# First attention of a transformer layer: the values become the standing operand, and the probabilities are divided by their sum before they are turned

## The reference, cut to what matters

```python
# group 0: |distance| <= 64; groups 1 and 2: the tokens of the same class (stride 4, stride 16)
sc = where(valid, einsum('qe,ke->qk', q, k) * 64 ** -0.5, -1e30)      # per group, per head
lse = logsumexp(sc); p = exp(sc - lse); o = p @ v                      # per group
o_a = sum_g softmax_g(lse)[g] * o[g]                                   # = one softmax over all groups' keys
# second branch: 8 query heads over 2 key heads, dense over 256 keys
o_b = softmax(q_b @ k_b.T * 64 ** -0.5) @ v_b
merged = sigmoid(gate0 + b0) * (o_a @ w_proj_a) + sigmoid(gate1 + b1) * (o_b @ w_proj_b)
x = x + merged @ w_out
# then rmsnorm, a router (top 4 of 32 experts), and the experts' swiglu
```

## Time and profile before

| what | value |
|---|---|
| median of three runs | 1928.79 us (1928.77 to 1929.28) |
| profiled execution, its own time | 1928.52 us |
| its span, first to last instruction | 1926.7 us |
| PE, DVE, ACT busy | 96%, 48%, 30% of the span |
| granted PE clock | 0.999 |
| read from memory | 558.08 MB, 290 GB/s over the span |

### The profile page before, as it was taken

How to read it: one execution, slowest core, us unless ns; L and a number is a source line. 1 busy time by engine, 2 the same in 40 slices (tenths; PEclk the granted TensorE clock), 3 DMA queues, 4 the chain that set the end, 5 groups by cost and what they waited for, 6 DMA issues and landing times.

```text
span 1926.7 us, 25464 instructions
## 1 busy us (share of the span) xinstructions
PE 1857.3 (96%) x10228; PEld 1110.0 (58%) x10228; DVE 917.1 (48%) x1607; ACT 584.1 (30%) x863; POOL 100.3 (5%) x120
## 2 busy tenths in 40 slices
PE   8999999999999999999999999999999999999998
PEld 5877874333333333233233333787888887878886
DVE  6864465323332333233232232676765455566544
ACT  3554442111111111111111111554435344555432
POOL 2410000000000000000000000020410000000000
PEclk9999999999999999999999999999999999999999
DMA  7543399999999999999999999542145455436452
GB/s 253 175 146 116 112 392 407 417 426 428 426 428 428 427 429 426 429 428 427 429 426 429 427 428 427 184 162 97 60 160 178 171 199 177 151 131 240 153 204 81
DMA packets 106464, 560.29 MB, mean 291 GB/s; under 512 B 5904, under 2 KB 11280, under 8 KB 81808
## 3 DMA queue, kind: packets, MB, share of 16 engines
q1 hardware_dynamic: 102528, 551.61, 71.2%
q10 hardware_dynamic: 3856, 7.53, 1.3%
HBM read 558.08 MB, written 1.05 MB: 290 GB/s over the span
## 4 chain that ended last, share of the span: by engine, by line
PE 71%; DMA 19%; DVE 4%; ACT 3%; issue 2%; POOL 1%; POOLq 0%; SPq 0%; ACTq 0%; DVEq 0%
PE ps L1297 14%; PE ps L948 11%; PE ps L949 11%; PE ps L950 11%; DMA ring<-in_w_gate_up_dram 10%; DMA arena<-in_w_gate_up_dram 8%; PE ps L1327 8%; PE ps L1226 2%; PE ps L1238 2%; PE ps L962 1%; PE ps L1312 1%; PE ps L1557 1%; DVE arena L2862 1%; PE ps L1434 1%; PE ps L984 1%
## 5 line engine op out<-in xcount | busy, mean ns | idle before, releaser
L1297 PE MATMUL ps<-ring,arena 128*64 128x512 f32 x1280 | 286.6, 596 | 23.8 <-DMA ring<-in_w_gate_up_dram 23.8
L2720 DVE TENSOR_SCALAR arena<-ps 128x512 f32<-128x512 f32 x32 | 22.1, 691 | 518.5 <-PE ps L1297 518.5
L2260 DVE TENSOR_TENSOR split_w<-ring,split_w 128x1024 fp32r<-128x1024 f32 (+2 forms) x176 | 203.9, 1205 | 81.9 <-ACT split_w L2054 81.3
L948 PE MATMUL ps<-split_w,act_parts 128*128 128x512 f32 (+1 forms) x544 | 209.7, 386 | 2.0 <-issue 1.0
L1297 PEld LDWEIGHTS ps<-ring,arena 128*64 128x64 f32 x1280 | 87.8, 137 | 209.9 <-issue 161.5
L950 PE MATMUL ps<-split_w,act_parts 128*128 128x512 f32 (+1 forms) x544 | 205.7, 378 | 0.0
L949 PE MATMUL ps<-split_w,act_parts 128*128 128x512 f32 (+1 forms) x544 | 205.3, 377 | 0.0
L2054 ACT ACTIVATE split_w<-ring 128x1024 fp32r<-128x1024 f32 (+2 forms) x176 | 171.7, 1033 | 110.1 <-PE ps L950 108.6
L1297 PE MATMUL ps<-arena 128*64 128x512 f32 x768 | 172.5, 595 | 10.6 <-DMA arena<-in_w_gate_up_dram 10.3
L1327 PE MATMUL ps<-ring,arena 128*64 128x512 f32 x720 | 160.6, 594 | 0.1
L1945 ACT ACTIVATE arena<-arena 128x512 f32<-128x512 f32 x32 | 20.2, 630 | 457.7 <-DVE arena L2720 457.7
(11 more groups left out here) (382 smaller groups left out, 2804.3 us busy)
## 6 DMA issues: line engine op xcount, KB each, us to landing
ring<-in_w_gate_up_dram SPq DMA_DIRECT2D x80, 2048.0 KB, 34.1
arena<-in_w_gate_up_dram SPq DMA_DIRECT2D x48, 2048.0 KB, 27.0
ring<-in_w_down_dram SPq DMA_DIRECT2D x45, 2048.0 KB, 33.7
ring<-in_f_w_dram SPq DMA_DIRECT2D x28, 2048.0 KB, 8.0
arena<-in_w_down_dram SPq DMA_DIRECT2D x19, 2048.0 KB, 37.2
ring<-in_w_in_dram SPq DMA_DIRECT2D x14, 2048.0 KB, 7.8
ring<-in_a_w_in_dram SPq DMA_DIRECT2D x6, 2048.0 KB, 8.1
ring<-in_b_w_qkv_dram SPq DMA_DIRECT2D x6, 2048.0 KB, 8.0
```

The costliest lines, as they stand in the source:

```text
L948: pe.matmul(dst, lh, rh, start=start, stop=False)
L1297: mm = pe.matmul(ps[half, bank, :], xeT[:, 2 * c + j, :], w[:, j, col:col + 512], start=False, stop=(c == 3 and j == 1), skip_group_check= ...
L2260: dve.tensor_tensor(part_place(load, 1, k, n)[:, s_, :], raw_place(load, k, n)[:, s_, :], part_place(load, 0, k, n)[:, s_, :], ALU.subtract)\
L2720: dve.tensor_scalar(gate_c, ps[:, 1, :], 7.0, None, ALU.min).then_inc(m_clipped, 1)
```

## The change

v becomes the standing operand and the turned probabilities the moving one, so the sums come out turned (head dimension on the partitions, queries along the free axis), and the turning after the last step is gone. The inverse of the sums can then no longer be applied to the result; DVE applies it to the probabilities ahead of the turn, in place. ACT takes the high part of each unit's sums and DVE the low part at once. v of groups 1 and 2 is kept so that group 1 fills partitions 0 to 63 and group 2 partitions 64 to 127 (`v_class`), which needs two copies of 64 partitions per tile, and lets one matmul per 64 queries and head cover both groups. The turned results lie in the arena over the place of the early chunk (`once_place`) and in a part of `late`, so these two transfers move behind the output projections. The rows of `w_proj_b` are put in another order on the host.

```diff
@@ sync
-            read_out(sync, G_PROJ - 1)
-            sync.dma_start(once_place, expert_weights(*divmod(ONCE, RING))).then_inc(mask_in, 16)
             load(OUT_LOAD, w_out3[:, :, 0:512])
-            sync.wait_ge(o_turned, 4)
+            sync.wait_ge(pv_done, UNITS)
             expert_chunk(0, 0, 0)
             load(OUT_LOAD + 1, w_out3[:, :, 512:1024])
             sync.wait_ge(pre_split, quarters_done(OUT_LOAD, 3))
             expert_chunk(1, 0, 1)
             sync.wait_ge(gemm_ready, G_PROJ + 8)
             expert_chunk(2, 0, 2)
+            read_out(sync, G_PROJ - 1)
+            sync.dma_start(once_place, expert_weights(*divmod(ONCE, RING))).then_inc(mask_in, 16)
@@ tensor
             def turn_probs(u):
-                pe.wait_ge(probs_ready, u + 1)
+                pe.wait_ge(probs_scaled, u + 1)
...
                 else:
                     for e in range(2):
-                        for j in range(2):
-                            pe.transpose(ps[:, 6 + e, j * P:(j + 1) * P],
-                                         probs_a[:, e, j * P:(j + 1) * P], ident)
-                    for e in range(2):
-                        for g in range(1, NG):
-                            for a in range(2):
-                                own = slice(CLASS * a, CLASS * a + CLASS)
-                                mm = pe.matmul(ps[own, 6 + e, keys_of(g)],
-                                               probs_a[own, e, keys_of(g)], ident[own, own],
-                                               start=True, stop=True, skip_group_check=True)
+                        for j in range(KEYS // P):
+                            mm = pe.transpose(ps[:, 6 + e, j * P:(j + 1) * P],
+                                              probs_a[:, e, j * P:(j + 1) * P], ident)
@@ weighted, dense units
-                    for kv in range(2):
-                        for kt in range(2):
-                            j = 2 * kv + kt
-                            mm = pe.matmul(ps[:, 5, S + 64 * kv:S + 64 * kv + 64],
-                                           probsT[:, j * P:(j + 1) * P],
-                                           v_b[:, kt, 64 * kv:64 * kv + 64], ...)
+                    for kt in range(2):
+                        for kv in range(2):
+                            j, q = 2 * kv + kt, slice(64 * kv, 64 * kv + 64)
+                            mm = pe.matmul(ps[q, 5, S:S + P], v_b[:, kt, q],
+                                           probsT[:, j * P:(j + 1) * P], ...)
@@ weighted, the other units
-                    for e in range(2):
-                        for kt in range(2):
-                            pe.matmul(ps[:, 5, out_at[e]], probsT_a[:, e, kt * P:(kt + 1) * P],
-                                      v_a[:, kt, v_at[e]], ...)
-                        for g in range(1, NG):
-                            for a in range(2):
-                                own = slice(CLASS * a, CLASS * a + CLASS)
-                                mm = pe.matmul(ps[own, 5, out_at[e]], probsT_a[own, e, keys_of(g)],
-                                               v_groups[own, g, v_at[e]], ...)
+                    for kt in range(2):
+                        for e, q in enumerate(head_rows):
+                            pe.matmul(ps[q, 5, S:S + P], v_a[:, kt, v_at[e]],
+                                      probsT_a[:, e, kt * P:(kt + 1) * P], ...)
+                    for a in range(2):
+                        own = slice(S + CLASS * a, S + CLASS * a + CLASS)
+                        for e, q in enumerate(head_rows):
+                            mm = pe.matmul(ps[q, 5, own], v_class[:, tile, a, v_at[e]],
+                                           probsT_a[:, e, own], ...)
@@ behind the last step
-            pe.wait_ge(o_ready, UNITS)
-            for b, o in enumerate((o_b, o_a)):
-                for tile in range(NT):
-                    for j in range(4):
-                        mm = pe.transpose(ps[:, 4 + 2 * b + tile, j * P:(j + 1) * P],
-                                          o[:, tile, j * P:(j + 1) * P], ident)
-                    mm.then_inc(o_turned, 1)
             for b in range(2):
                 for tile in range(NT):
-                    pe.wait_ge(oT_ready, 2 * b + tile + 1)
+                    pe.wait_ge(o_ready, (PAIR_UNITS, UNITS)[b])
@@ scalar
+                    elif kind == "v_a" and group == 0:
+                        act.activation(v_a[:, tile, :], ps[:, bank, :], ACT.Copy)\
+                            .then_inc(gemm_free[bank], 1)
                     elif kind == "v_a":
-                        act.activation(v_a[:, tile, group * 512:(group + 1) * 512], ps[:, bank, :],
-                                       ACT.Copy).then_inc(gemm_free[bank], 1)
+                        at = slice(CLASS * (group - 1), CLASS * group)
+                        for a in range(2):
+                            own = slice(CLASS * a, CLASS * a + CLASS)
+                            ins = act.activation(v_class[at, tile, a, :], ps[own, bank, :], ACT.Copy)
+                        ins.then_inc(gemm_free[bank], 1)
...
                 elif event[0] == "attend":
                     i = event[1]
+                    if 0 <= i - 2 < UNITS:
+                        act.wait_ge(pv_done, i - 1)
+                        act.activation(oT_of(0, i - 2), ps[:, 5, S:S + P], ACT.Copy)\
+                            .then_inc(oT_high, 1)
...
-            for b in range(2):
-                for tile in range(NT):
-                    act.wait_ge(o_turned, 2 * b + tile + 1)
-                    act.activation(oT_parts[:, 0, b, :, tile * P:(tile + 1) * P], ...)
...
-            act.dma_start(late[:, :], t["late"]).then_inc(late_in, 16)
...
+            act.wait_ge(gemm_ready, G_PROJ + 8)
+            act.dma_start(late[:, :], t["late"]).then_inc(late_in, 16)
@@ vector, a step
-                    u = i - 2
-                    if 0 <= u < UNITS:
-                        dve.wait_ge(pv_done, u + 1)
-                        after(inverted[u])
...
-                            dve.tensor_tensor(dst, ps[:, 5, S:S + 128]..., inv[:, :, None]..., ALU.mult)
                     u = i - 1
                     if 0 <= u < UNITS:
                         dve.wait_ge(probs_ready, u + 1)
-                        if u >= 2:
-                            dve.wait_ge(o_ready, u - 1)
-                        inverted[u] = step.on(dve.reciprocal(inv_sum[:, 2 * (u % 2):2 * (u % 2) + 2],
-                                                          psum_[:, 0:2]))
+                        after(step.on(dve.reciprocal(inv_sum[:, 0:2], psum_[:, 0:2])))
+                        for e in range(2):
+                            x = probs[:, S * e:S * e + S] if u < PAIR_UNITS else probs_a[:, e, :]
+                            ins = dve.tensor_scalar(x, x, inv_sum[:, e:e + 1], None, ALU.mult)
+                        ins.then_inc(probs_scaled, 1)
+                    u = i - 2
+                    if 0 <= u < UNITS:
+                        dve.wait_ge(oT_high, u + 1)
+                        dve.tensor_tensor(oT_of(1, u), ps[:, 5, S:S + P], oT_of(0, u),
+                                          ALU.subtract).then_inc(o_ready, 1)
@@ vector, behind the last step
-            for b in range(2):
-                for tile in range(NT):
...
-                    dve.tensor_tensor(oT_parts[:, 1, b, :, s_], ..., ALU.subtract).then_inc(oT_ready, 1)
```

More of the change, by code:

```diff
@@ L352 @@
 PRE_QUARTERS = 4 * (PRE_LOADS - FULL_LOADS)
-PRE_HIGHS = 12
+PRE_HIGHS = 8
 MOBA_CHUNKS = [("k", 0), ("q", 0), ("v", 0), ("k", 1), ("q", 1), ("v", 1)]
@@ L402 @@
 ONCE = 8
+OT_AT = 17920
 ONCE_AT = 17408
@@ L436, in program @@
         base = sb("base", [P, C_END])
+        with ExitStack() as late_scope:
+            late_scope.enter_context(nc.sbuf_tensor("ahead_of_oT", [P, NT * KEYS], F32))
+            oT_late = late_scope.enter_context(nc.sbuf_tensor("oT_late", [P, 2, S], F32R))
         late = sb("late", [P, L_END])
@@ L698, in program, with oT, oT_of @@
         w_dn = t["w_down"].rearrange("e (c p j) n -> e c p (j n)", c=2, p=P)
+        def oT(part_, b, k):
+            i = 8 * b + 4 * part_ + k
+            return oT_arena[:, i, :] if i < 14 else oT_late[:, i - 14, :]
+        def oT_of(part_, u):
+            b, unit_ = divmod(u, PAIR_UNITS)
+            pair, tile = divmod(unit_, 2)
+            return oT(part_, b, pair)[:, tile * P:(tile + 1) * P]
         def slot(i, k, n):
@@ L1053, in weighted @@
                     pe.wait_ge(v_ready, 2)
[L1054 to L1060 removed]
+                    for kt in range(2):
+                        for kv in range(2):
+                            j, q = 2 * kv + kt, slice(64 * kv, 64 * kv + 64)
+                            mm = pe.matmul(ps[q, 5, S:S + P], v_b[:, kt, q],
+                                           probsT[:, j * P:(j + 1) * P], start=(kt == 0),
+                                           stop=(kt == 1), skip_group_check=True)
                 else:
```

(33 more changed lines are left out.)

36 lines of the change are left out of this document (6 added, 30 removed).

## The result

The changed kernel takes 1949.91 us (1947.85 to 1953.0, 4 runs) against 1929.03 us (1928.77 to 1930.81, 4 runs) for the kernel before: ratio 1.0104, 95% interval [1.0092, 1.0116], 20.9 us more. The forecast was 1944, range 1936 to 1950: the direction and the main mechanism came as forecast, the size is 0.1 us inside the range's upper edge, and two of the four runs lie above it (1950.92 and 1953.0). The profiled execution took 1950.92 us, its span 1949.0 (before 1926.7), granted PE clock 0.993. One of the runs of filler (experiment 4) was a slow one, 2539.69 us at a granted clock of 0.696, and is left out of its median.

A forecast was written before the change was run, and what follows sets the result against it. The prediction took the expert stage's end to hang on when the unbroken stream of weight transfers starts, behind the attention. A first issue 12.7 us later plus 3.0 for a break gave 15.7 on 1928.52: 1944 us, range 1936 to 1950.

The forecast's parts named there:

- The lateness of the scores: Attention: each unit's scores fall behind the kernel before as turns wait for DVE's scaling, summing to 13.8 us by unit 15.
- The scaling's price: DVE in each attention step: two tensor_scalar ops of 0.30 or 0.37 us, a pair taking 0.52 or 0.67.
- the rival at one result a cycle: DVE's scaling runs at one result a cycle, 5 us more in the attention: 1949 us; chance 12%.
- Unit 3: Dense attention step two halves on: PE sets the pace and the chain ends at about the same time, 0 us late.
- The gate-stage cycle: Attention units 11 to 15, two halves apart: 10.57 us a step against 9.73, together +4.2 us.
- Behind the attention: From the last half to the first load of the weight stream: first issue at 252.9, 12.7 us later.
- The break: Transfer stream after its first issue: only two loads queued, so the engines stand idle and lose 3.0 us in all.
- The case that I gave 52%: The forecast as it stands, whole kernel: 1944 us, its own range 1941 to 1947.
- PE sets the pace, and it has less to do: Rival, attention units 9 to 15: PE saves 1.1 us a step, 9.3 earlier less 3.0 for the break, 1922; chance 7%.
- The break costs nothing: Rival, transfer stream: the attention is late by 12.7 us but the stream's idle time adds nothing, 1941; chance 20%.
- Partly paid: Rival, attention: only the dense steps lose, 6.4 us, and half the end comes back, 4 to 6 late, 1933; chance 6%.
- no change: Rival, whole kernel: gain and loss cancel, 1929 us; chance 3%.

The follow-up runs named there:

- filler: The changed kernel, with PE doing 4 or 7 small useless matmuls ahead of each unit's turns, where it would wait for the scaling; 1945.95 us.
- experiment 4: The changed kernel with small useless PE matmuls ahead of the turns, run twice: 1945.95 and 1944.98 us; the changed kernel beside the latter 1949.95.
- after_again: The changed kernel as it is, measured again beside the second run of useless matmuls on PE; 1949.95 us.
- filler_again: The changed kernel with the same useless PE matmuls ahead of the turns, measured a second time beside the changed kernel on one chip; 1944.98 us.
- before_scaled_early: The kernel before, with DVE scaling into an unused place right behind the negative peak, ahead of the low quarter, and the turn waiting for it; 1930.19 us.
- scale_early: The changed kernel with only DVE's inverse and scaling moved right behind the unit's negative peak, ahead of the low quarter; 1919.32 us.
- before_scaled: The kernel before, with DVE scaling into an unused place behind its inverse and the turn waiting for it, no operand swap; 1965.9 us.
- before_loads: The kernel before, with only the early chunk and the mask transfer moved behind the output projections as in the change; 1929.29 us.
- early_first: The changed kernel with early scaling, the third expert chunk loaded early and w_out's first half issued behind both chunks; 1921.9 us.
- early_between: The changed kernel with early scaling, the third expert chunk loaded early and w_out's first half issued between the two chunks; 1918.75 us.
- early_chunk: The changed kernel with early scaling, and the third expert chunk's load moved ahead of w_out's second half; 1919.06 us.
- chunk: The changed kernel, scaling left where it was, with only the third expert chunk's load moved ahead of w_out's second half; 1950.05 us.

## Why the prediction was right, and where its size was off

**What bounds the kernel: right.** The end of the expert stage hangs on "when the unbroken stream of transfers starts". From the first issue to the experts' last sum the profiles of five kernels have nearly one number, whatever the attention took (after_again and filler_again: 961.4 each):

| kernel | first issue | experts' last sum | between |
|---|---|---|---|
| before | 240.18 | 1200.90 | 960.7 |
| before_scaled_early | 240.06 | 1201.08 | 961.0 |
| after | 259.61 | 1220.95 | 961.3 |
| filler | 254.44 | 1215.69 | 961.3 |
| scale_early | 229.72 | 1190.20 | 960.5 |

In before_scaled, which is 33 us late, it is 963.0. Where the order of the first loads was changed it is another: 964.6 in before_loads (1200.85 - 236.23), 967.7 in early_first (1193.70 - 225.96), 964.0 in early_between (1189.19 - 225.24), 958.7 in early_chunk (1189.76 - 231.04), 961.8 in chunk (1222.40 - 260.62). So a later attention moves the end by as much, within 0.6 us for these five and 2.3 for before_scaled; but an earlier start alone is not an earlier end: early_between starts 3.3 earlier than scale_early and ends the stage at the same time (anchored 1076.6 and 1076.4).

**The lateness of the scores, step by step.** Anchored; peaks up to unit 7, scores from unit 8, in us behind the kernel before:

| up to unit | forecast | after | filler |
|---|---|---|---|
| 1 | 2.0 | 2.1 | 2.1 |
| 7 | 6.4 | 8.0 | 8.1 |
| 8 | 7.6 | 9.4 | 9.4 |
| 10 | 9.6 | 13.1 | 11.8 |
| 15 | 13.8 | 21.2 | 17.4 |

- *The scaling's price was too low.* One op of 128x256 took 350 ns and one of 128x384 took 418, by line and form:

```profile
L2442 DVE TENSOR_SCALAR arena<-arena,small 128x384 f32<-128x384 f32 x16 | 6.0, 418 | 0.3
L2442 DVE TENSOR_SCALAR arena<-arena,small 128x256 f32<-128x256 f32 x16 | 4.9, 350 | 0.3
```

  I had 0.30 and 0.37, so the pairs took 0.62 and 0.75 instead of 0.52 and 0.67. The kind was right (the rival at one result a cycle, 1949, is out although its time is nearest to what came): 128 elements more cost 68 ns, and the 754 ns of the earlier trace rows lie on the same line, 0.21 us + 0.53 ns per element. Ops with two tensors take 1.04 ns per element (422 ns at 256 in the earlier trace rows, 1222 at 1024 for the low quarter). The fixed part is 0.21 us and not the 0.15 that I took from a small op. The Trainium skill, "VectorE: DVE Perf Modes", "Mode 2×_2P — use both read ports for one tensor", gives such a one-tensor op in fp32 two results a cycle and one with two tensors one. The trace agrees: the two slopes, 0.53 and 1.04, stand in that ratio. Worth 0.1 a step, some 1.4 over the steps.
- *Unit 3 was not free.* Forecast 0, measured +0.7 (3.9 after unit 3, 3.2 after unit 2): there the two limits did not coincide, and PE waited 0.24 and 0.52 us for DVE.
- *The gate-stage cycle* at full clock was 10.7 and 11.1 by turns (filler: 179.95, 190.65, 201.76, 212.45, 223.57) against 10.57, 1.5 over five steps, 0.4 of it the scaling's price once more. These three together are 3.2 of the 3.6 us (17.4 - 13.8) by which filler, at full clock, missed the forecast.
- *The clock was missing.* The step of the prediction that failed is its sum for the steps behind the gates, "+ 0.20 + 0.67 + 0.05 + 0.75 = 10.57": it makes PE wait in each of them and still counts turns, scores and halves at the durations of a PE that never waits. Measured, four of the five cycles from unit 10 to 15 are 11.1 to 11.9 us, one is 10.7. It costs 3.8 us up to unit 15 (21.2 - 17.4) and 5.2 at the first issue (259.61 - 254.44): by its size nearly all of the distance between forecast and result (filler, without it, takes 1945 to 1946). The profile of chunk, whose attention is the changed kernel's, is a third point between the two: three stretches of 3.4 us at half clock up to unit 15 (10.2 us together, against 17.1 in the changed kernel and none in filler), and 19.3 us late there against 21.2 and 17.4.

```profile
163.00:230.00 67.00, 53.30 (x406) 39.31 (x405) 30.61 (x74) 28.15 (x55) 0.00 (x0) 0.94 0.29 99
```

  The Trainium skill has the pattern in "TensorE: Matmul & The Clock Gate", "HAM oscillation — how this bites in real kernels": waits between groups of matmuls make each group start at half rate, on top of the wait. The trace agrees in part: a group at 0.50 behind a wait at 190 to 194, but not behind every wait, and the page's example has longer waits, for transfers. A change that makes a fully busy PE wait in every step should have brought that rule to mind.

**Behind the attention.** Forecast +12.7 for the first issue from a lateness of 13.8; measured 21.7 from 21.2, so the end cost 0.5 more where I had 1.1 less (the first projection began at 259.88, forecast 252.9). In filler, at full clock, it gave back 1.0 (16.5 from 17.4), so most of this too is the clock, which is at half in 249.5 to 252.9. **The break** was forecast at 3.0. The idle in the two windows is 1.0 and 1.6 us (0.48 x 2 and 0.52 x 3), but the stream's whole loss against before is 0.6 (961.3 - 960.7). The bytes came back: in the 48 us behind the start the changed kernel moved 380 GB/s against 397, in the next 55 us 423 against 411 (each counted from 1.8 us behind the first issue). The likely reason is that the displaced transfers had cost something where they stood before, which I had not asked; no run moves one of them alone, so it is not shown. **Behind the experts** I forecast a mere shift; there is 1.6 us of half clock in one block (14.6 us against 12.99). after_again, both fillers and early_between have it too (14.5 to 14.6, chunk and before_scaled 15.8 and 15.9), scale_early, early_chunk, early_first, before_scaled_early and before_loads do not (12.99). What brings it about was not tested and is open.

Sum as measured in the spans: 19.4 + 0.6 + 0.7 + 1.6 = 22.3, against 12.7 + 3.0 = 15.7.

**Luck.** That the clock's 5.2 us come so near to the 5.9 by which 1944 was short is partly luck. Anchored, the sum was short by 8.9 (24.6 - 15.7): 5.2 for the clock, 3.6 for what filler missed as well, 2.3 behind the experts and 0.2 elsewhere, less 2.4 that the break did not cost. Of this the profiled execution won back 2.3 by its early start. With the 0.6 that the break cost in place of 3.0 the forecast would have been 1942, eight us under what came. The case that I gave 52% had the range 1941 to 1947, and the result lies outside it.

**The rivals.** "PE sets the pace, and it has less to do" named the right condition, a chain under 8.9 us a step, and its price: 1922 forecast, 1919.3 measured when the scaling is early, and a first issue 9.7 earlier anchored, against 9.3. It had its parts a little off: the dense steps lost 1.5, the sums with v standing save more than the 0.65 that I gave them. From one step of each kernel they take 1.83 us before (177.10 to the turns at 178.93) and 0.82 now (193.00 to 193.82), the turns 1.20 and 0.81. The first row of the sums before:

```profile
177.10 0.55 PE L1071 MATMUL ps<-arena 128*128 128x64 f32 x4
```

My reason against this rival, that the order of DVE's list forbids it, held for this kernel and not for scale_early. The advice of the Trainium skill, "TensorEngine Tiling (Array Packing)", "When to Use Tiling", to swap where the moving side has 64 columns, is thus borne out for PE's time (8.43 against 9.73 us a step, 0.4 of it from fewer turns), and only if the scaling it brings forward is kept off the path. "The break costs nothing" was near the truth as a mechanism (0.6 in the profiles, up to 2 in before_loads), wrong with its time, since the attention's lateness was mis-sized. "Partly paid" and "no change" are out.

## What to carry to other kernels

When a division moves from the result to an operand, it moves onto the path from the softmax to the next product: put it where its input is ready and the engine idles, here right behind the exponentials, and not where the old one stood. The place of some 0.9 us of work a step, in the list of an engine that goes through it in order, was worth 30 us between two otherwise equal kernels (1919.3 and 1949.9). And where a new wait cuts into a busy PE, add the half-clock stretches behind it to the price; here they were 5 of 21 us.

## What the runs showed of the hardware

- In the changed kernel, of the eight waits of PE for the scaling behind the gates, the five of 2.17 to 2.60 us (ending at 171.3, 191.1, 203.4, 225.3, 248.2) each had a stretch at half clock (0.50) beside them. It began between 0.4 us ahead of the wait's end and 1.7 behind it, and lasted 3 to 7 us. The waits of 0.52, 0.71 and 1.83 and those of 1.4 in the dense steps had none. This is no rule by length: the first wait, of 2.46 at 117.3, had none either, one of 2.20 in chunk (ending at 174.4) had none, and in before_scaled six waits of 1.25 to 1.49 had one each. The fall can come behind work at full clock: the turns at 203.40 still took 0.87, and the clock fell at 205.1. Small products in the waits kept the clock at 1.00 in 163 to 230 in both profiles of filler.
- Where the stream of transfers had 2.5 us of idle time near its start, it lost 0.6 us up to its end: 380 GB/s instead of 397 in the first 48 us, 423 instead of 411 in the next 55. Why the later rate was the higher one was not tested.
